# Sample attention unrolled over four staggered pairs, with the block ranking inside the prompt loop

## What is computed

```python
s_c = einsum('bgrqd,bgcd->bgrqc', qh, kc) * scale + tab[bucket(d_c)]
p_c = masked_softmax(s_c, d_c >= 0)          # 63 compressed blocks a sample
o_c = einsum('bgrqc,bgcd->bgrqd', p_c, vc)
imp = einsum('bgrqc,cj->bgqj', p_c, cover)   # 17 selection blocks
imp = where(forced, 1e9, ...)
_, idx = lax.top_k(imp, 16)                  # 16 of the 17 are kept
o_s = softmax(q . ks[idx] + bias) . vs[idx]  # selected, up to 1024 + 8 keys
o_w = softmax(q . kw + bias) . vw            # window, 512 + 8 keys
o = g[0] * o_c + g[1] * o_s + g[2] * o_w
```

## Time and profile before

| | us |
|---|---|
| median of 3 runs | 1505.13 |
| lowest, highest | 1499.01, 1505.28 |
| the profiled execution | 1500.33 |
| its span in the profile | 1498.7 |
| TensorE, VectorE, ScalarE, GpSimd busy | 1354.9, 571.7, 433.7, 207.2 |
| prompt loop | 722.9 to 810.6 |
| mixer and sample stage | 810.6 to 967.4 |

### The profile page before, as it was taken

The page is one execution under the profiler, slowest core; times in us unless marked ns, Lnnn a source line. Parts: engine busy times, 40 slices in busy tenths (PEclk is TensorE's granted clock), DMA queues, the critical chain, the costliest instruction groups (busy, mean ns, idle before and its releaser), DMA issues.

```text
span 1498.7 us, 27290 instructions
## 1 busy us (share of the span) xinstructions
PE 1354.9 (90%) x10212; PEld 1235.1 (82%) x10212; DVE 571.7 (38%) x975; ACT 433.7 (29%) x692; POOL 207.2 (14%) x402
## 2 busy tenths in 40 slices
PE   4999999999999979987688577597999999999996
PEld 3899999999999979855465444497999999999995
DVE  2422222223333551144774233458333333333355
ACT  2222222222111342254465122224322222221123
POOL 3000000000000253340801133103200000000010
PEclk9999999999999989999699677697999999999996
DMA  9454544545443447544101331021222222222321
GB/s 301 132 165 119 165 144 136 168 123 154 134 133 105 88 113 159 127 117 162 45 2 33 99 105 48 26 85 43 71 84 84 84 84 84 84 63 83 86 64 63
DMA packets 249163, 156.03 MB, mean 104 GB/s; under 512 B 46188, under 2 KB 242552, under 8 KB 249032
## 3 DMA queue, kind: packets, MB, share of 16 engines
q1 hardware_dynamic: 240415, 136.42, 32.2%
q0 software_dynamic: 6384, 17.79, 4.1%
q10 hardware_dynamic: 2304, 1.05, 0.2%
HBM read 150.86 MB, written 8.60 MB: 106 GB/s over the span
## 4 chain that ended last, share of the span: by engine, by line
PE 77%; DVE 7%; issue 5%; SPq 4%; ACT 3%; DMA 2%; DVEq 1%; POOL 1%; POOLq 1%; ACTq 0%
PE ps L304 59%; PE ps L773 2%; PE ps L1771 2%; PE ps L1146 1%; PE ps L1262 1%; DVE AR L1804 1%; SPq L1738 1%; PE ps L782 1%; PE ps L281 1%; SPq L1737 1%; PE ps L1136 1%; PE ps L1163 1%; DVE XT L467 1%; POOL AR L1028 1%; PE ps L366 1%
## 5 line engine op out<-in xcount | busy, mean ns | idle before, releaser
L304 PE MATMUL ps<-UH,WH 128*128 128x288 f32 x1680 | 363.1, 297 | 8.6 <-DVE WL L264 4.9
L304 PE MATMUL ps<-UL,WH 128*128 128x288 f32 x1680 | 358.9, 295 | 0.0
L304 PE MATMUL ps<-UH,WL 128*128 128x288 f32 x1680 | 358.5, 294 | 0.0
L264 DVE TENSOR_TENSOR WL<-RAW,WH 128x1024 fp32r<-128x1024 f32 x159 | 197.2, 1241 | 416.6 <-ACT WH L260 411.0
L304 PEld LDWEIGHTS ps<-UH,WH 128*128 128x128 f32 x1680 | 269.6, 189 | 9.8 <-DVE WL L264 5.6
L304 PEld LDWEIGHTS ps<-UL,WH 128*128 128x128 f32 x1680 | 271.1, 188 | 0.0
L304 PEld LDWEIGHTS ps<-UH,WL 128*128 128x128 f32 x1680 | 269.8, 188 | 0.0
L260 ACT ACTIVATE WH<-RAW 128x1024 fp32r<-128x1024 f32 x159 | 167.2, 1053 | 226.1 <-PE ps L304 202.6
L503 POOL TENSOR_TENSOR AR<-AR 128x576 f32<-128x576 f32 x18 | 29.5, 1637 | 939.2 <-ACT AR L414 874.2
L304 PE MATMUL ps<-HH,WH 128*128 128x288 f32 x704 | 152.4, 298 | 2.9 <-DVE HL L655 2.7
L304 PE MATMUL ps<-HH,WL 128*128 128x288 f32 x704 | 151.2, 295 | 0.0
(11 more groups left out here) (318 smaller groups left out, 1401.1 us busy)
## 6 DMA issues: line engine op xcount, KB each, us to landing
RAW<-in_w_ffn_in_dram SPq DMA_DIRECT2D x88, 512.0 KB, 5.1
AW<-in_w_ada_dram SPq DMA_DIRECT2D x56, 512.0 KB, 4.3
RAW<-in_w_ffn_out_dram SPq DMA_DIRECT2D x32, 448.0 KB, 3.7
RAW<-in_w_ffn_out_dram SPq DMA_DIRECT2D x16, 512.0 KB, 3.9
AR<-in_w_ada_dram SPq DMA_DIRECT2D x7, 1024.0 KB, 11.0
RAW<-in_w_in_dram SPq DMA_DIRECT2D x28, 256.0 KB, 4.2
AR<-in_cache_k_cmp_dram POOLq DMA_DIRECT2D x64, 64.0 KB, 2.8
AR<-in_cache_v_slc_dram POOLq DMA_DIRECT2D x64, 64.0 KB, 2.1
```

The source lines that it names most:

```text
L264: nc.vector.tensor_tensor(WL[:, slot, :], RAW[:, slot, :], WH[:, slot, :].bitcast(F32), ALU.subtract).then_inc(split_done, 1)
L304: mm = nc.tensor.matmul(ps[:, 2 * uslot + h, 0:HT], W[:, wslot, k * P:(k + 1) * P], R[:, k0 + k, h * HT:(h + 1) * HT], start=(first and k ...
```

## The change

**In the prompt loop.** `sample_cmp_pe`, `sample_cmp_act` and `sample_cmp_dve` do the compressed scores, their softmax and the ranking of all four pairs at once, in bank 7, one piece behind each of the steps 1 to 12. The prompt's values now all go to bank 6; `o_evac` moves ahead of the exponentials of its step, and TensorE waits for it (`o_a`) at every fourth step.

**After the loop.** All engines are unrolled over the four pairs. Banks 4, 5 and 6 are one ring of fills (`FILLS`), evacuated by ScalarE or VectorE (`on_act`): keys of pair 0 and 1, mixer, then weights of a pair and keys of the pair after next. TensorE's order is: keys 0, scores 0, keys 1, mixer, then for each pair p its weights, the scores of p+1, the values of p, the keys of p+2. The gate and the softmax sum are multiplied into the weights before they are turned (`sample_weight`). The values are stationary and the turned weights move (L1261 to L1269), so the output, one [128 x 64] a sample, is summed over the three branches in bank 7 and already turned; ScalarE copies it out (`sample_out`). New keys, queries and compressed keys are read in place, not copied.

**Buffers and loads.** Two key buffers (`KA`, and `KB` over `WH`/`WL`), three value buffers (`VA` over `RAW`, `VB`, `VC`). SP loads keys 0 and 1 and values 0 during the prompt loop, keys 2 after the turn of keys 0, keys 3 after that of keys 1, then the first two `w_out` chunks after `sav_done` 1, then half of values 3. GpSimd loads values 1 from the end of the loop, values 2 after the mixer and values 1, half of values 3 after `sav_done` 2. The first `w_out` split moves to the stage's end, `hi` behind `sample_out(2)`, `lo` ahead of the evacuation of the last weights.

```diff
+            for p in range(2):
                 for b in range(2):
+                    window_load(sp, state_k_win, KWIN[p], p, b, k_full[p])
                     for j in range(NPG):
...
+                        slc_page(sp, cache_k_slc, KPG[p], p, b, j, k_full[p])
+            sp.wait_ge(split_done, CH0["w_in"] + 14 + 3)
+            for b in range(2):
+                window_load(sp, state_v_win, VWIN[0], 0, b, v_sp)
...
+            for p in range(2, 4):
+                sp.wait_ge(r_t, fill("K", p - 2, 5) + 1)
...
+            sp.wait_ge(sav_done, 1)
+            out_load(0, 0)
+            out_load(0, 1)
+            sp.wait_ge(sav_done, 2)
+            window_load(sp, state_v_win, VWIN[3], 3, 0, v_sp)
...
+            pool.wait_ge(r_t, fill("M", 3, 1) + 1)
+            pool.wait_ge(v_pool, V_PAIR)
...
+                for b in range(2):
+                    out, at = ps[:, 7, 64 * b:64 * b + 64], 64 * b
+                    nc.tensor.matmul(out, VCN[0:CS, 2 * p + b, :], SPCG[0:CS, p * P + at:p * P + at + 64], start=True, stop=False)
+                    for j in range(NPG):
+                        nc.tensor.matmul(out, VPG[p][:, b, j, :], SPT[:, j * P + at:j * P + at + 64], start=False, stop=False)
...
+            turn_probs(0)
+            sample_scores(1)
+            sample_values(0)
+            turn_keys(2)
+            turn_probs(1)
+            sample_scores(2)
+            sample_values(1)
+            turn_keys(3)
+            turn_probs(2)
+            sample_scores(3)
+            sample_values(2)
+            turn_probs(3)
+            sample_values(3)
...
+            for p in range(4):
+                sample_weight(p, 0)
+                sample_weight(p, 1)
+                if p < 3:
+                    drop_block(p + 1)
...
+                else:
+                    lo(dve, *split_args("w_out", 0)[:2])
+                prob_evac(dve, p, 1)
+                prob_evac(dve, p, 3)
```

More of the change, by code:

```diff
@@ L1342, in attn_act @@
                     pt_evac(act, u - 1, 0)
+                if u % 4 == 1 and u > 1:
+                    o_evac(act, u // 4 - 1)
                 if u < NU:
@@ L1416, in attn_dve @@
             a = "w_in"
-            for j in range(1, 15):
+            for j in range(1, 14):
                 n, slot, _f = split_args(*next_chunk(a, j))
@@ new lines, in build @@
+        VB = (v5["VB"][:, 0:2 * PAST], v5["VB"][:, 2 * PAST:])
+        VC = (AR1[:, oG - 1584 - 512:oG - 1584 - 512 + 2 * PAST], AR3[:, 2 * WCH:3 * WCH])
+        assert CH0["w_out"] % 2 == 1
+        KPG, KWIN = ([pages(v[q]) for v in (KA, KB, KA, KB)] for q in range(2))
+        VPG, VWIN = ([pages(v[q]) for v in (VA, VB, VC, VB)] for q in range(2))
+        K_PAIR = V_PAIR = 16 * 2 * (NPG + 1)
+        SSUM, WS = RS[:, 512:514], RS[:, 514:516]
+        NMA, NMB, NMS, NMW = (RS[:, 516 + k:517 + k] for k in range(4))
@@ new lines, in build, with fill @@
+        cmp_mm, cmp_v, cmp_a = sem("cmp_mm"), sem("cmp_v"), sem("cmp_a")
+        sav_done, so_a, uh_tail = sem("sav_done"), sem("so_a"), sem("uh_tail")
+        FILLS = [("K", 0, k) for k in range(6)] + [("K", 1, k) for k in range(6)]
+        FILLS += [("M", g, h) for g in range(4) for h in range(2)]
+        for q in range(4):
+            FILLS += [("T", q, k) for k in range(4)]
+            FILLS += [("K", q + 2, k) for k in range(6)] if q < 2 else []
+        def fill(kind, q, k):
+            return FILLS.index((kind, q, k))
@@ new lines, in on_act, with ring_bank, evac_wait, ring_wait @@
+        def on_act(f):
+            kind, q, k = FILLS[f]
+            if kind == "M":
+                return 2 * q + k >= 3
+            return k != 3 if (kind, q) == ("K", 1) else k % 2 == 0
+        def ring_bank(f):
+            return 4 + f % 3
+        def evac_wait(eng, f):
+            eng.wait_ge(r_a if on_act(f) else r_d, sum(on_act(q) == on_act(f) for q in range(f + 1)))
+        def ring_wait(pe, f):
+            if f >= 3:
+                evac_wait(pe, f - 3)
+            elif ring_bank(f) == 6:
+                pe.wait_ge(o_a, REP)
```

594 lines of the change are left out of this document (323 added, 271 removed).

## The result

The changed kernel takes **1431.63 us** (median of 4 runs, 1426.01 to 1434.66), the kernel before in the same comparison 1502.07 us: a ratio of 0.953, 95% interval [0.949, 0.957]. The forecast was 1429 us, between 1412 and 1449. The profiled execution took 1429.57 us, its span is 1427.4 us, 71.3 less than before.

| stretch | before | after | difference | forecast |
|---|---|---|---|---|
| start to prompt loop | 722.9 | 722.9 | 0 | 0 |
| prompt loop | 87.7 | 94.1 | +6.4 | +6 |
| sample stage | 156.8 | 80.9 | -75.9 | -77.2 |
| the rest | 531.3 | 529.6 | -1.7 | 0 |

A forecast was written before the change was run, and what follows sets the result against it. Bound: a sample stage of 156.8 us that no engine works through, about half at 1.2 GHz, with values waiting on one buffer. Stage -84.2, clock +7, ranking +6: -71.2 from 1500.3 gives 1429 us; range 1412 to 1449.

The forecast's parts named there:

- Loads: Sample stage: SP issues a key pair in 20 us; key pair 3 lands 45 us after T0, the prompt loop's end.
- Rival 2: Sample stage: the loads bind, a page taking 1.45 us in place of 1.19; 1438 us, chance 0.12.
- TensorE's work: Sample stage at 2.4 GHz: 66.2 us in all, of which values 28.4, priced by their weight loads.
- rival 3: Sample stage: value products follow their moving columns, 3.7 us a pair; 1422 us, chance 0.08.
- The waits that stay: Sample stage: waits remaining at the start, for key pair 3 and before the last values, which end at 72.6 us.
- The ring at the start: Start of the sample stage: the three banks of fills cost TensorE about 3 us.
- the keys: Sample stage: after the values of pair 1, TensorE waits for key pair 3 from +43.4 to +45.2 us.
- the split: Late sample stage: w_out's first split precedes the last weight evacuations, so TensorE waits from 63.5 to 65.4 us.
- The clock: Sample stage: two episodes of 7 us at half speed after short waits, +7 us; bounds 0 and 23.
- the turned operands buy nothing per product: Sample stage's value products: stationary values cost 7.1 us a pair, against 7.4 before.
- Rival 1: Sample stage: clock stays low, half the stage at 1.2 GHz, +23 in place of +7; 1445 us, chance 0.20.
- The ranking: Prompt loop: block ranking moved inside adds 6 us, between 0 and 11.

The follow-up runs named there:

- experiment 1: Changed kernel with each value product moving all 128 columns of turned weights instead of 64: 1419.51 us, ratio to before 0.946.
- experiment 4: Changed kernel with values moving again (128 columns) and 64 weight columns stationary, plus a copy and transpose per pair: 1420.38 us, ratio to before 0.945.
- experiment 7: w_out's first split moved behind the last weight evacuations: on the changed kernel 1431.71 us; with value products also moving 128 columns 1416.10 us.
- experiment 2: Changed kernel with each value product moving only 32 columns, half the sample attention's output columns left out: 1430.72 us.
- experiment 8: Changed kernel with 128 moving columns, later w_out split, and some pages of key pair 3 and value pair 3 swapped between SP and GpSimd: 1414.02 us.
- experiment 3: Changed kernel with value products moving 128 columns for pairs 0 and 2, 64 for pairs 1 and 3: 1418.98 us.
- experiment 6: Changed kernel with the three value buffers acting as one: 1472.37 us; in a second kernel the two key buffers acting as one: 1460.60 us.
- experiment 5: Changed kernel with the whole block ranking placed behind the prompt loop instead of inside it: 1440.64 us.

## Why the prediction was right, and where it wasn't

**Loads: right.** The last issue of key pair 3 was forecast at T0+43.3 and came at T0+40.7; no pair's keys or values made TensorE wait. The margin was thin, and only the low clock made it: at full clock the same keys are late by 1.1 to 3.0 us (experiments 1, 4, 7). Rival 2, that the loads bind, was closer than the profile after alone would tell, but its cause, slower pages, did not come: SP took 18.8 us for the 16 pages and two windows of a pair, 1.17 us a page with the windows counted in.

**TensorE's work: right within 2 us.** From the full-clock rows: keys 11.6 (12.8 forecast), scores 11.8 (13.2), mixer 4.3, weights 6.5 (7.5), values 30.2 (28.4), 64.4 in all (66.2). Taking the weight load as the price of a value product was right; rival 3, the moving columns, is out by experiment 2 too.

**The waits that stay: oversized.** Forecast 3 us at the start, 1.8 for the keys and 1.9 for the split, 6.4 with the rest; measured 0.3, 0 and 0.8. The ring at the start cost nothing. The other two exist, but the slower clock hid them until experiment 1 uncovered them at 1.1 and 2.05 us.

**The clock: the step that failed.** The term "two episodes of 7 us at half speed, 3.5 us each: +7" had the wrong mechanism and half the size. There were four, which cost 15.4 us in all. Three began in the second sample's value products, in unbroken work, the fourth in the first sample's of the last pair, 2 us behind the wait of 0.80; with 128 columns the first three don't happen at all (experiments 1 and 8), and with both widths in one run the fall is where the 64 columns are (experiment 3). The prediction took its episodes from the earlier trace rows, and for the kernel before it read them rightly: there the low window from 847 to 854 us comes from what is ahead of it, not from the value products. The clock had fallen by 845.6 us, behind a wait of 1.90 and before the first value product at 847.27:

```profile
844.56 1.50 PE L1242 MATMUL ps<-IDN,AR 128*128 128x128 f32 x8 [1.90 <-ACT AR L1384]
```

```profile
845.60:847.20 1.60, 1.05 (x5) 0.18 (x3) 0.82 (x3) 0.60 (x1) 0.00 (x0) 0.50 0.26 75
```

Those products move 128 columns, and in experiment 4 the same form holds the full clock. The failed step was to carry the price over to products of another form, which the change itself brought in. The prediction's statement that "the turned operands buy nothing per product" held (0.115 us a record), but it priced the product's time alone and put its effect on the clock at nothing. Rival 1 (+23) was as far off as the forecast's +7: the measured 15.4 us lie half way between them. The mean clock of 0.80 is nearer to its "below 0.8" than to the forecast's 0.9, but its cause, that the stage's operations are those of the kernel before, isn't what the experiments show. The Trainium skill (page "TensorE: Matmul & The Clock Gate", section "Part 4: PE-mode transpose") says that the clock does not rise for transposes. Here 24 of them behind full-clock products ran in 2.97 us (experiments 1, 3 and 8), and behind 14 us of low clock the clock rose while only they ran (experiment 6). The traces don't agree with the page there.

So the sum was right to 3 us by luck: two errors cancelled, 7 us too much work and waiting against 8 too little clock.

**The ranking: the number right, its parts not.** +6 forecast, +6.4 measured, of which the ranking itself makes some 4.5 (experiment 5). TensorE's own records of it, 26 records of products and 8 transposes, take 4.0 us, as the prediction had them before it multiplied by the chain's share and charged 2.4. VectorE's operations, charged at 3.7, add 0.5 to 0.7 us of waiting. TensorE's wait for VectorE's weights did rise, from 6.4 to 8.8 us, but 8.3 of that stay when the ranking is taken out, so another part of the change causes the rise; which, these runs don't show. The rest of the difference is the clock at the loop's start. VectorE's rows of the ranking in the loop (busy, mean ns, idle before), against the 0.25 to 0.35 us that the prediction took; all 16 together are 4.9 us, where it had 5.5:

```profile
L1825 DVE TENSOR_TENSOR RS<-ps,AR 128x252 f32<-128x252 f32 x1 | 0.6, 568 | 0.0
L1830 DVE TENSOR_TENSOR RS<-RS 128x252 f32<-128x252 f32 x1 | 0.4, 422 | 0.1
```

## What to carry to other kernels

When the rows show that a product's price is its weight load, ask also what that form of product does to the clock: columns that cost no time can be worth having for it, and fewer of them cost this stage 9.8 of 80.9 us. For a window with a low clock, look at the moment where it *fell*, and not only inside the window: a full engine at 1.2 GHz can be the tail of a wait (845.6 us in the kernel before, experiment 1's 3.68 us) or of unbroken work (841 us in the changed kernel), and an edit of the work alone, as in experiment 1, shows whether it is the cause. And a slow engine covers waits of its partners: whoever restores its speed should already know the next load that will be late.

## What the hardware showed unexpectedly

- The granted clock fell to 1.2 GHz in unbroken TensorE work with 128 stationary columns and 64 moving. Of 15 pairs of such value products that began at full clock (the changed kernel, experiments 3, 5, 6 and 7), 14 lost it before they ended; of 18 with 128 moving columns (experiments 1, 3, 4, 7 and 8) one did, right behind 2.05 us of waits. The stage's mean was 0.76 to 0.80 with 64 in an unbroken stage, 0.98 to 1.00 with 128. What the chip counts, these runs don't tell.
- A float32 product's record took 0.112 to 0.118 us at full clock with 128 stationary columns and 32, 64 or 128 moving, and also with 64 stationary and 128 moving where a sample's products all write to the same half of the output rows (experiment 4). By the Trainium skill (same page, section "LDWEIGHTS (loading the stationary operand)") the load's time follows its columns, 107 ns for 128, which fits; for 64 it would be 53 ns. The 0.112 us isn't the price of 64 stationary columns as such, though: in the prompt loop products of that form go to the two halves in turn, and eight records (L1179) take 0.58 us (815.05 to 815.63), 0.073 each; eight of the small scores (L1218, 8 moving), also in turn, take 0.25 us, 0.031 each. Whether the two samples of a pair taken in turn would run at 0.073 wasn't tried; by an estimate from these rows that is worth 60 x 0.039 = 2.3 us a pair.
- Two queues issuing pages side by side did not slow each other. SP took 18.8 us for the keys of a pair during the prompt loop, when GpSimd issued nothing (740.44 to 759.27), and 18.8 beside it (819.96 to 838.77); GpSimd's pages started 1.17 us apart. The DMA engines moved 208 GB/s from 858 to 866 us.
